# The start of a two-block kernel: x fetched with features in partitions, its squares summed as a tree, other fillers on TensorE

## The reference, cut to what matters

```python
def rms_norm(x, g):
    xf = x.astype(jnp.float32)
    y = xf * lax.rsqrt(jnp.mean(xf * xf, axis=-1, keepdims=True) + EPS)
    return (y * g.astype(jnp.float32)).astype(x.dtype)

def mamba2_layer(x, norm_g, w_in, conv_w, conv_b, dt_bias, a_log, d_skip, gate_norm_g, w_out):
    h = rms_norm(x, norm_g)
    zxbcdt = h @ w_in                    # 1024 -> 2048 + 4096 + 32
    z = zxbcdt[..., :SSM_D_INNER]
    xbc = zxbcdt[..., SSM_D_INNER:SSM_D_INNER + SSM_CONV_DIM]
    dt_raw = zxbcdt[..., SSM_D_INNER + SSM_CONV_DIM:]
    xbc = jax.nn.silu(causal_depthwise_conv(xbc, conv_w, conv_b))
    dt = jax.nn.softplus(dt_raw + dt_bias)
    ...
    return x + y @ w_out
```

## Time and profile before

| | |
|---|---|
| time, median of 3 runs | 1215.8 us (1215.69 to 1215.84) |
| the profiled execution's own time | 1215.64 us |
| its span, first to last instruction | 1214.0 us |
| TensorE busy | 1203.9 us (99%) |
| VectorE busy | 910.2 us (75%) |
| ScalarE busy | 669.9 us (55%) |
| GpSimd busy | 52.1 us (4%) |

### The profile page before, as it was taken

One profiled execution on the slowest core, in us unless ns is written; L12 is line 12 of the kernel. 1 busy time (PEld: TensorE's weight loads), 2 busy tenths in 40 slices (PEclk: granted clock), 3 DMA queues, 4 the chain that ended last, 5 costly groups with the idle time before them and its releaser, 6 DMA issues.

```text
span 1214.0 us, 18151 instructions
## 1 busy us (share of the span) xinstructions
PE 1203.9 (99%) x6685; PEld 1004.0 (83%) x6685; DVE 910.2 (75%) x1406; ACT 669.9 (55%) x1098; POOL 52.1 (4%) x46
## 2 busy tenths in 40 slices
PE   9999999999999999999999999999999999999997
PEld 6788888888888887878787789847899888999886
DVE  5888889888965357667777789998798434786776
ACT  6566756675664253656556473775577421577222
POOL 1001210112010000000000000000000000000000
PEclk9999999999999999999999999999999999999999
DMA  6434333423324323222222232123332432332322
GB/s 173 134 97 121 82 110 104 119 71 109 116 70 130 104 78 90 77 70 69 69 69 80 77 87 73 50 70 104 104 105 70 150 93 73 101 106 91 117 89 102
DMA packets 168059, 115.42 MB, mean 95 GB/s; under 512 B 3376, under 2 KB 161360, under 8 KB 166976
## 3 DMA queue, kind: packets, MB, share of 16 engines
q1 hardware_dynamic: 166112, 104.02, 28.9%
q0 software_dynamic: 1888, 10.62, 2.6%
HBM read 112.46 MB, written 2.16 MB: 94 GB/s over the span
## 4 chain that ended last, share of the span: by engine, by line
PE 96%; DVE 2%; DMA 1%; issue 0%; ACT 0%; SPq 0%; ACTq 0%
PE psum L659 54%; PE psum L1192 11%; PE psum L1289 6%; PE psum L929 4%; PE psum L861 4%; PE psum L1035 3%; PE psum L1090 2%; PE psum L898 2%; PE psum L916 1%; PE psum L765 1%; PE psum L773 1%; PE psum L756 1%; PE psum L910 1%; PE psum L747 1%; PE psum L741 1%; PE psum L1104 1%
## 5 line engine op out<-in xcount | busy, mean ns | idle before, releaser
L1325 ACT ACTIVATE w_hi<-w_raw 128x1024 fp32r<-128x1024 f32 x156 | 164.7, 1056 | 275.8 <-PE psum L659 198.6
L2001 DVE TENSOR_TENSOR w_lo<-w_raw,w_hi 128x1024 fp32r<-128x1024 f32 x156 | 190.5, 1221 | 107.8 <-ACT w_hi L1325 107.0
L659 PE MATMUL psum<-a_hi,w_hi 128*128 128x512 f32 (+1 forms) x640 | 227.1, 375 | 0.2
L659 PE MATMUL psum<-a_lo,w_hi 128*128 128x512 f32 (+1 forms) x640 | 222.3, 368 | 0.0
L659 PE MATMUL psum<-a_hi,w_lo 128*128 128x512 f32 (+1 forms) x640 | 221.5, 367 | 0.0
L659 PE MATMUL psum<-b_hi,w_hi 128*128 128x512 f32 x376 | 150.0, 399 | 0.2 <-DVE w_lo L2734 0.2
L659 PE MATMUL psum<-b_lo,w_hi 128*128 128x512 f32 x376 | 148.6, 395 | 0.0
L659 PE MATMUL psum<-b_hi,w_lo 128*128 128x512 f32 x376 | 148.0, 394 | 0.0
L659 PEld LDWEIGHTS psum<-a_hi,w_hi 128*128 128x128 f32 x640 | 115.3, 188 | 24.0 <-issue 3.9
L659 PEld LDWEIGHTS psum<-a_hi,w_lo 128*128 128x128 f32 x640 | 115.1, 188 | 20.7
L659 PEld LDWEIGHTS psum<-a_lo,w_hi 128*128 128x128 f32 x640 | 115.0, 188 | 19.1
(11 more groups left out here) (398 smaller groups left out, 2556.4 us busy)
## 6 DMA issues: line engine op xcount, KB each, us to landing
w_raw<-a_w_in SPq DMA_DIRECT2D x48, 512.0 KB, 3.9
w_raw<-w_down SPq DMA_DIRECT2D x32, 512.0 KB, 4.0
arena<-acs POOLq DMA_DIRECT2D x8, 1024.0 KB, 5.0
w_raw<-a_w_out SPq DMA_DIRECT2D x16, 512.0 KB, 4.1
w_raw<-w_kv SPq DMA_DIRECT2D x16, 512.0 KB, 3.7
w_raw<-b_w_in SPq DMA_DIRECT2D x16, 512.0 KB, 3.9
w_raw<-w_in SPq DMA_DIRECT2D x14, 512.0 KB, 3.8
arena<-w_up SPq DMA_DIRECT2D x7, 1024.0 KB, 5.3
```

What stands on the lines that cost most here:

```text
L659: ins = mm(out, wv[:, u.par, k, :], xv[:, k0 + k, c0:c0 + cn], start=(first and begin and i == 0 and n == 0), stop=(last and end and i == ...
L1325: ac(w_hi[:, u.par, :, :], w_raw[:, u.par, :, :], ACT.Copy).then_inc(S["hi_ready"], 1)
L2001: tt(w_lo[:, u.par, :, :], w_raw[:, u.par, :, :], f32(w_hi[:, u.par, :, :]), ALU.subtract).then_inc(S["lo_ready"], 1)
```

## The change

x now comes from the host transposed (`x_t`, features as rows), and SP loads it in four parts of two feature blocks straight into `h`, behind the norm's parameters (which came on POOL's queue) and T0's weights; T1's weights, the dt weights and the identity follow. TensorE's 32 transposes and the copies into `h` go. ScalarE squares the eight blocks in two instructions of four blocks each, with hi(T1) and hi(T2) behind them; VectorE adds the blocks as a tree (four adds of 2, 2, 2 and 1 blocks); TensorE sums over partitions with four products against a column of ones into bank 7, just before the last block of T1. The spread of the reciprocal root moves from the middle of T1 to behind the first block of T2. TensorE's fillers on zeros become nine at the start and three between T0 and T1. T0 to T5 get four banks (`FIRST_BANKS`) in place of two. On VectorE, in the first group, lo(T3) moves ahead of `time_steps`, and lo(T4) ahead of taps 1.

```diff
+FIRST_BANKS = (1, 0, 3, 2, 1, 0)
+WARM = 9
+SPREAD = 1
...
-        x_tok = place(NT, D, at=0)
+        x_sq = place(KT, SEQ, at=0)
@@ SP @@
+            sp.dma_start(par[:, C_ANORM:C_KVN], t["params"][:, C_ANORM:C_KVN]).then_inc(S["anorm_in"], 16)
+            load(Lin(U_MAMBA), t["a_w_in"], 0, ssd_cols(Lin(0))[0])
+            for i in range(4):
+                sp.dma_start(h[:, 2 * i:2 * i + 2, META:T2], t["x_t"].rearrange("(k p) s -> p k s", p=P)
+                             [:, 2 * i:2 * i + 2, :]).then_inc(S[f"x_in{i}"], 16)
+            load(Lin(U_MAMBA + 1), t["a_w_in"], 0, ssd_cols(Lin(0))[1])
+            sp.dma_start(wdt, t["w_dt"]).then_inc(S["raw0"], 16)
             sp.dma_start(ident, t["consts"][:, K_ID:K_ID + P]).then_inc(S["con_in"], 16)
-            for i in range(4):
-                if i == 1:
-                    load(Lin(U_MAMBA), t["a_w_in"], 0, ssd_cols(Lin(0))[0])
-                if i == 3:
-                    sp.dma_start(wdt, t["w_dt"]).then_inc(S["raw0"], 16)
-                sp.dma_start(x_tok[:, :, 256 * i:256 * i + 256], t["x"].rearrange("(t p) d -> p t d", p=P)
-                             [:, :, 256 * i:256 * i + 256]).then_inc(S[f"x_in{i}"], 16)
-            group(Lin(0), 1)
+            group(Lin(0), 2)
@@ POOL @@
-            pool.dma_start(par[:, C_ANORM:C_KVN], t["params"][:, C_ANORM:C_KVN]).then_inc(S["anorm_in"], 16)
...
-            pool.wait_ge(S["xsum_ready"], NT)
-            pool.wait_ge(S["x_tp"], KT)
+            pool.wait_ge(S["x_tp"], 1)
@@ TensorE @@
-            warm(4).then_inc(S["unit_done"], 1)
-            pe.wait_ge(S["con_in"], 16)
-            def turn_x(ks):
...
+            warm(WARM).then_inc(S["unit_done"], 1)
...
-            for k in (0, 2, 4):
-                turn_x((k, k + 1))
-                if k < 4:
-                    warm(1)
             u, m = Lin(U_MAMBA), Lin(M_MAMBA)
-            tile_of(u, m, a_hi, a_lo, False, ks=range(2), ready=("x_lo", 1))
-            turn_x(range(6, KT))
-            tile_of(u, m, a_hi, a_lo, False, ks=range(2, KT), ready=("x_lo", 3))
+            tile_of(u, m, a_hi, a_lo, False, ready=("x_lo", 1))
+            warm(3, 7)
             u, m = u + 1, m + 1
             tile_of(u, m, a_hi, a_lo, False, ks=range(3))
             pe.wait_ge(S["dtw_ready"], 1)
             dt_products()
             tile_of(u, m, a_hi, a_lo, False, ks=range(3, 5))
-            pe.wait_ge(S["rs_ready"], 1)
-            spread(bank(4), stat_at(X_RS), TOKENS1, S["rb_ready"])
-            tile_of(u, m, a_hi, a_lo, False, ks=range(5, KT))
+            tile_of(u, m, a_hi, a_lo, False, ks=range(5, 7))
+            pe.wait_ge(S["x_cpv"], 4)
+            sums(bank(7), x_sq[:, 0, :], TOKENS1, S["x_tp"])
+            tile_of(u, m, a_hi, a_lo, False, ks=range(7, KT))
...
             def first_group(j, ks=range(KT)):
-                tile_of(Lin(U_MAMBA + j), Lin(M_MAMBA + j), a_hi, a_lo, False, ks=ks)
+                tile_of(Lin(U_MAMBA + j), Lin(M_MAMBA + j), a_hi, a_lo, False, ks=ks,
+                        free=M_MAMBA if j < 4 else M_MAMBA + j - 3, out=bank(FIRST_BANKS[j]))
...
-            first_group(2)
+            first_group(2, range(SPREAD))
+            pe.wait_ge(S["con_in"], 16)
+            pe.wait_ge(S["rs_ready"], 1)
+            spread(bank(4), stat_at(X_RS), TOKENS1, S["rb_ready"])
+            first_group(2, range(SPREAD, KT))
@@ ScalarE @@
+            hi(Lin(U_MAMBA))
             act.wait_ge(S["anorm_in"], 16)
-            turned_high((0, 1))
-            hi(Lin(U_MAMBA))
-            turned_copies((1,))
-            turned_high((2, 3, 4, 5))
...
-            token_squares(0)
-            turned_high((6, 7))
-            hi(Lin(U_MAMBA + 1))
-            turned_copies((3, 5, 7))
-            for i in range(1, NT):
-                token_squares(i)
-            act.wait_ge(S["xsum_ready"], NT)
+            turned_high(range(KT))
+            for k in (0, 4):
+                ac(x_sq[:, k:k + 4, :], h[:, k:k + 4, META:T2], ACT.Square).then_inc(S["xsum_ready"], 1)
+                hi(Lin(U_MAMBA + 1 + k // 4))
             own.wait()
-            root(stat_at(X_SD), stat_at(X_SUM), eps1, 1.0 / D, S["xsd_ready"])
-            hi(Lin(U_MAMBA + 2))
+            act.wait_ge(S["x_tp"], 1)
+            root(stat_at(X_SD), bank(7)[:, 0:NT], eps1, 1.0 / D, S["xsd_ready"])
@@ VectorE @@
-            turned_low((0,))
-            turned_copies((0,))
-            turned_low((1,))
             lo(Lin(U_MAMBA))
-            turned_low(range(2, KT))
+            turned_low(range(KT))
+            def add_blocks(to, off):
+                tt(x_sq[:, to:to + off, :], x_sq[:, to:to + off, :], x_sq[:, to + off:to + 2 * off, :], ALU.add
+                   ).then_inc(S["x_cpv"], 1)
+            dve.wait_ge(S["xsum_ready"], 1)
+            add_blocks(0, 2)
             lo(Lin(U_MAMBA + 1))
             dve.wait_ge(S["raw0"], 32)
             tt(wdt, wdt, par[:, C_ANORM:C_ANORM + KT].unsqueeze(2).to_broadcast([P, KT, 32]), ALU.mult
                ).then_inc(S["dtw_ready"], 1)
-            turned_copies((2, 4, 6))
+            dve.wait_ge(S["xsum_ready"], 2)
+            add_blocks(4, 2)
+            dve.wait_ge(S["x_cpv"], 2)
+            tt(x_sq[:, 0:2, :], x_sq[:, 0:2, :], x_sq[:, 4:6, :], ALU.add).then_inc(S["x_cpv"], 1)
+            dve.wait_ge(S["x_cpv"], 3)
+            add_blocks(0, 1)
...
-            dve.wait_ge(S["xsd_ready"], 1)
-            nc.vector.reciprocal(stat_at(X_RS), stat_at(X_SD)).then_inc(S["rs_ready"], 1)
...
             cp(dts[0], bank(5)).then_inc(S["dt_pre"], 1)
             lo(Lin(U_MAMBA + 2))
+            dve.wait_ge(S["xsd_ready"], 1)
+            nc.vector.reciprocal(stat_at(X_RS), stat_at(X_SD)).then_inc(S["rs_ready"], 1)
             dve.wait_ge(S["rt_ready"], 1)
...
             evacuate_in(g, 0)
+            lo(u + 3)
             time_steps()
             taps_of(g, 0)
             evacuate_in(g, 1)
-            lo(u + 3)
+            lo(u + 4)
             taps_of(g, 1)
             evacuate_in(g, 2)
-            lo(u + 4)
             dve.wait_ge(S["dt_exp"], 2)
...
-        "x": x["x"][0], "a_w_in": x["a_w_in"][0], "a_w_out": x["a_w_out"][0], "w_kv": x["w_kv"],
+        "x_t": x["x"][0].T, "a_w_in": x["a_w_in"][0], "a_w_out": x["a_w_out"][0], "w_kv": x["w_kv"],
```

More of the change, by code:

```diff
@@ L638, in tile_of @@
             def tile_of(u, m, xh, xl, wide, k0=0, first=True, last=True, ks=range(KT), ready=None,
-                        begin=None, end=None, lo="lo_ready", free=None, mark=None):
+                        begin=None, end=None, lo="lo_ready", free=None, mark=None, out=None):
                 begin = ks[0] == 0 if begin is None else begin
@@ L652, in tile_of @@
                 else:
-                    outs = [(acc(m), 0, SEQ)]
+                    outs = [(acc(m) if out is None else out, 0, SEQ)]
                 for i, k in enumerate(ks):
@@ L657, in tile_of @@
                     for n, (wv, xv) in enumerate(((w_hi, xh), (w_hi, xl), (w_lo, xh))):
-                        for out, c0, cn in outs:
-                            ins = mm(out, wv[:, u.par, k, :], xv[:, k0 + k, c0:c0 + cn],
+                        for o, c0, cn in outs:
+                            ins = mm(o, wv[:, u.par, k, :], xv[:, k0 + k, c0:c0 + cn],
                                      start=(first and begin and i == 0 and n == 0),
@@ L680, in _, with warm @@
             TOKENS1 = TOKENS2[:NT]
-            def warm(n):
+            def warm(n, b=1):
                 for _ in range(n):
-                    ins = mm(bank(1)[:, 0:256], rt[:, 0:P], rt[:, P:P + 256], start=True, stop=True,
+                    ins = mm(bank(b)[:, 0:256], rt[:, 0:P], rt[:, P:P + 256], start=True, stop=True,
                              skip_group_check=True)
@@ L690, in _, with dt_products @@
             pe.wait_ge(S["warm_set"], 1)
-            warm(4).then_inc(S["unit_done"], 1)
-            pe.wait_ge(S["con_in"], 16)
-            def turn_x(ks):
-                for k in ks:
+            warm(WARM).then_inc(S["unit_done"], 1)
+            def dt_products():
+                for k in range(KT):
                     if k % 2 == 0:
                         pe.wait_ge(S[f"x_in{k // 2}"], 16)
[L699 to L710, removed]
                     c = slice(32 * (k % 4), 32 * (k % 4) + 32)
@@ L825, in _ @@
             pe.wait_ge(S["dt_tok"], 1)
-            pe.wait_ge(S["x_cpa"], 4)
             pe.wait_ge(S["tab_in"], 16)
@@ L1338, in turned_high @@
                 for k in ks:
-                    act.wait_ge(S["x_tp"], k + 1)
-                    ac(a_hi[:, k, 0:SEQ], bank(2 + k % 6), ACT.Copy,
+                    act.wait_ge(S[f"x_in{k // 2}"], 16)
+                    ac(a_hi[:, k, 0:SEQ], h[:, k, META:T2], ACT.Copy,
                        scale=par[:, C_ANORM + k:C_ANORM + k + 1]).then_inc(S["x_hi"], 1)
[L1343 to L1350, removed]
             act.wait_ge(S["consts_set"], 5)
             own(ac(stat_at(X_SD, 1), one, ACT.Sqrt))
```

(37 more changed lines are left out.)

1 line of the change is left out of this document (added).

## The result

The changed kernel takes 1223.92 us (median; 1223.49 to 1225.23), the kernel before 1215.82 in the same comparison (1215.69 to 1216.01). The ratio is 1.0069, with a 95% interval of 1.0056 to 1.0081. So it is 8.1 us slower; forecast were 1223.2 us, and a chance of 0.88 for slower. The profiled execution took 1225.23 us, with a span of 1223.5.

What follows compares the result with a forecast made beforehand. TensorE, with 96% of the span, was taken to bound the kernel. Late root and VectorE's new order start T5 at 50.9 instead of 43.34, +7.6 us on the profiled 1215.64: 1223.2 us, no clock fall included, range 1220 to 1227.5.

Steps and rivals of the forecast that it cites:

- x and T0: Kernel start: last quarter of x lands at 11.5 (11.4 to 12.5) instead of 12.54; T0 ends near 14.4, before 17.8.
- T0's last operands: Behind the last x: 0.04 + two ScalarE steps + two VectorE steps (0.75 each), put at about 2.2 us.
- T1 and T2: First products on TensorE: T1's at 17.2 instead of 17.77, T2's at 26.0 against 26.17, about even.
- The root: Row of reciprocal roots rt, gating every evacuation of the first group: ready at 28.1 instead of 24.59, 3.5 us later.
- VectorE's order: First group: lo(T3) ends at 31.95 with T3 unharmed, lo(T4) at 41.3, lo(T5) at 50.8; T5 starts at 50.9.
- third wait for dt: In T5 on TensorE: none, since the steps of dt are ready at 53.3 and wanted at 53.7.
- the clock: TensorE's granted clock in the two waits: no fall in the sum; a fall would cost at most some 3 us, taken 1.5.
- The first wait: TensorE, through T3 at 37.8, waits 3.6 us for lo(T4), which ends at 41.3.
- the two falls of the rival: TensorE's clock falls in one wait or both: 1224.7 or 1226.2 us, bounds 1223.2 to 1229.2; chance 0.20.
- the second wait: TensorE, through T4 at 47.0, waits 3.9 us for lo(T5), which ends at 50.8.
- The rival that the order doesn't bind: VectorE's first group: no wait follows; 1215.5 us, or 1214 if x lands at 10; chance 0.12.
- x no sooner: Load of x at the start: lands at 12.5, all behind it moves by 1.0, 1224.2 us; chance 0.10.

Runs made afterwards that it cites:

- early root, new order: The changed kernel with VectorE's new order kept, sums right behind the dt products and the root's spread behind T1's fifth block: 1221.55 us, ratio 1.0049.
- order put back: The changed kernel with lo(T3) and lo(T4) back behind the evacuations of T1 and T2, as in the kernel before: 1218.69 us, ratio 1.0025.
- order alone: The kernel before with only lo(T3) moved ahead of time_steps and lo(T4) ahead of taps 1: 1219.99 us, ratio 1.0036.
- T1's weights first: The changed kernel with early root and old VectorE order, further changed: hi(T1) ahead of the squares, lo(T1) ahead of the adds; 1216.19 us, ratio 1.0000.
- old order, zeros before T3: The changed kernel with VectorE's order of before, late root, and five products on zeros in TensorE's wait before T3: 1218.35 us, ratio 1.0020.

## Why the prediction was right

Step by step, by its own numbers:

- **x and T0.** Last x 11.5 forecast; POOL was released at 11.63 by the row that stood at 12.54. The new runs moved at 393 GB/s from 5 to 10 us, above the 385 taken as the fast end. T0 ended at 14.48, as forecast (14.4 to 15.5). In the other traces with the new x and this order of loads POOL's row stands between 11.17 and 11.88, so a hit to 0.1 us is partly chance. The terms written for T0's last operands make 2.7 us and not the 2.2 that the forecast used; from the last x (3.44 + 7.90 = 11.34) to the last a_lo (9.40 + 4.13 = 13.53) it was 2.19, because the steps of ScalarE and VectorE overlap.
- **T1 and T2.** 17.2 and 26.0 forecast, 17.04 and 26.02 measured. The Square over 128x2048 took 1.90; the Exp of that shape that stood in for it has 1.92.
- **The root.** rt ready at 28.1 forecast, 27.50 + 0.60 = 28.10 measured.
- **VectorE's order.** lo(T3) to end at 31.95, T3 unharmed: 31.96 and 32.11. Evacuation 1 to end at 36.3: 36.25. hi(T4) 3.74 us behind it: 38.95 + 1.04 = 39.99, so 3.74. lo(T4) to end at 41.3: 41.26; TensorE's wait 3.6: 3.46. lo(T5) to end at 50.8, T5 at 50.9: 50.77 and 50.91. No third wait for dt.

The rows of ScalarE behind the hole (its timeline, after) show what fills it: the tap, silu's table load and the silu stand between evacuation 1 and hi(T4).

```profile
36.29 0.82 ACT L1351 ACTIVATE arena<-arena,gconv 128x512 f32<-128x512 f32 x1 [0.87 <-DVE arena L2066]
37.12 1.28 ACT L1362 ACT_TABLE_LOAD   x1
38.42 0.63 ACT L1362 ACTIVATE arena<-arena 128x512 f32<-128x512 f32 x1
38.95 1.04 ACT L1313 ACTIVATE w_hi<-w_raw 128x1024 fp32r<-128x1024 f32 x1
```

With ScalarE's order as it is, nothing shortens this. But hi(T4) itself wants only its weights (loaded behind lo(T2), which ended at 23.13, in 3.7 us) and the slot of T2, with which TensorE was through at 32.11. No run puts hi(T4) ahead of the table load, so that way out stays untried.

**The step that failed is the clock.** The prediction took one idle stretch, that at the end of the kernel, as a bound: both waits are shorter, so the sum has no fall. The first wait came as forecast, and the clock fell behind both in the profiled execution. That cost less than the two falls of the rival (3.0 us): T4's fall is hidden, since lo(T5) came only at 50.77, after T4 was through; it shortened the second wait from the forecast 3.9 to 2.30 us. Only T5's is paid, 1.64 us, where the prediction had taken 1.5 for a fall. With zeros in the waits the clock stays at 1.00 and the changed kernel takes 1223.45, so its median holds 0.5 us of falls. Its four executions went from 1223.49 to 1225.23 and only the slowest was traced, so how many of the others had a fall is not shown. The Trainium skill (TensorE: Matmul & The Clock Gate, "Why this matters for your kernels") warns of idle gaps over some 3 us between bursts. The wait of 3.46 us agrees with it, the one of 3.69 us without a fall (early root, new order) does not, and the falls behind 2.19 us (order put back) and 2.30 us came behind shorter gaps than those it names.

The rival that the order doesn't bind is refuted by both kernels that have the new order and an early root. x no sooner is refuted by 11.63.

## What to carry to other kernels

An operand's preparation moved up a queue that is worked in order makes all behind it late if its own input comes late: compare when that input is ready (here hi on ScalarE, behind a table load) with where the instruction now stands. A row that gates all evacuations sets, by way of their queue, the time of every feeder behind them. An earlier input won nothing here, where the preparation of the next operand (hi and lo of T1) sets the start.

## What was not expected of the hardware

- The granted clock did not follow the length of the wait alone: about half behind waits of 2.19 us (order put back, order alone), 2.25 us (the broadcast ahead of x), 2.30 and 3.46 us (the change), 1.00 behind one of 3.69 us. In the change the first fall came at 41.0, still within the wait, and the second near 51.2, some 0.3 us after T5's first product.
- A 16 KB broadcast to 128 partitions, put ahead of x on SP's queue, took 5.3 us and held back the first a_hi by 2 us (8.99 instead of 7.02); the windows from 5 to 10 us moved 299 GB/s with it, 393 in the changed kernel.
- A step of a_hi took 0.72 us from h in SBUF (the change) and 0.69 us from the banks of PSUM (before), medians of eight.
- The load of 1 MB for the MLP near 900 us took 5.1 to 5.7 us in ten of the thirteen traces, and 6.3 (the change), 6.2 (T1's weights first) and 7.3 us (old order, zeros before T3) in three. Just these three have a wait of TensorE behind it in the MLP, of 0.5, 0.4 and 1.5 us. What decides it stays open.
